# Fifteen checks with constants in place of a register loop, on four engines, for the spare expert blocks

## The reference, cut to what matters

```python
def grouped_expert_ffn(x2d, expert, gate, w_gate, w_up, w_down):
    # assignments sorted by expert, laid out in 128-row blocks that each belong to one expert
    ...
    def expert_block(args):
        xblk, e = args
        h = jax.nn.silu(xblk @ w_gate[e]) * (xblk @ w_up[e])
        return h @ w_down[e]
    yb = lax.map(expert_block, (xb, blk_expert)).reshape(cap, dm)
    y = yb[dest] * sgate[:, None]
    return jnp.zeros_like(x2d).at[stok].add(y)
```

## Time and profile before

| | before |
|---|---|
| median of 3 runs | 3962.31 us |
| span of the profiled execution, first to last instruction | 3962.9 us |
| instructions in it | 40374 |
| TensorE busy with matmuls | 3711.2 us, 94% of the span |
| VectorE, ScalarE, GpSimd busy | 42%, 19%, 4% |
| mean granted TensorE clock | 0.971 |

### The profile page before, as it was taken

One profiled execution on the slowest core, in us unless ns is written; L12 is line 12 of the kernel. 1 busy time (PEld: TensorE's weight loads), 2 busy tenths in 40 slices (PEclk: granted clock), 3 DMA queues, 4 the chain that ended last, 5 costly groups with the idle time before them and its releaser, 6 DMA issues. The chain is left out here.

```text
span 3962.9 us, 40374 instructions
## 1 busy us (share of the span) xinstructions
PE 3711.2 (94%) x15836; PEld 2158.0 (54%) x15836; DVE 1664.2 (42%) x2996; ACT 764.9 (19%) x1713; POOL 172.2 (4%) x393
## 2 busy tenths in 40 slices
PE   8988899989889999999789999999998999999999
PEld 4654787745344345555345454488444545448844
DVE  0118533555232011111445564554464655355435
ACT  1202211211132111000224352110002435110000
POOL 1001000000100000000202000000000200000000
PEclk9989999998999999999899999999999999999999
DMA  8542012223779887887441112222223110221221
GB/s 319 181 168 97 26 54 97 85 110 138 305 287 381 330 353 307 316 326 283 168 125 43 45 55 88 75 85 85 85 87 113 43 60 26 74 100 60 86 95 53
DMA packets 199024, 576.39 MB, mean 145 GB/s; under 512 B 24612, under 2 KB 34644, under 8 KB 185832
## 3 DMA queue, kind: packets, MB, share of 16 engines
q1 hardware_dynamic: 178064, 515.15, 34.8%
q10 hardware_dynamic: 12888, 32.14, 2.3%
q0 software_dynamic: 7888, 26.53, 1.9%
HBM read 541.80 MB, written 32.00 MB: 145 GB/s over the span
## 5 line engine op out<-in xcount | busy, mean ns | idle before, releaser
L346 PE MATMUL ps<-out_sums 128*128 128x256 f32 (+1 forms) x1152 | 333.6, 450 | 2.3 <-issue 2.3
L346 PEld LDWEIGHTS ps<-out_sums 128*128 128x128 f32 x1152 | 219.0, 190 | 113.9 <-issue 94.4
L346 PE MATMUL ps<-ring,mixers_xT 128*128 128x256 f32 (+2 forms) x1024 | 254.0, 403 | 14.1 <-DMA ring<-in_w_in 7.2
L346 PEld LDWEIGHTS ps<-ring,mixers_xT 128*128 128x128 f32 x1024 | 195.9, 201 | 61.3 <-issue 22.0
L346 PE MATMUL ps<-mixers_xT,ring 128*128 128x512 f32 (+1 forms) x480 | 209.2, 594 | 2.7 <-DMA ring<-in_w_in 1.7
L346 PE MATMUL ps<-ring,layers_hT 128*128 128x512 f32 x416 | 185.8, 604 | 17.2 <-PEq L276 16.2
L2307 PE MATMUL ps<-ring,mixers_xT 128*64 128x512 f32 x416 | 183.5, 598 | 2.1 <-issue 1.1
L346 PE MATMUL ps<-ring,ctx_hT 128*128 128x512 f32 (+2 forms) x448 | 168.9, 536 | 11.3 <-PEq L276 10.3
L2308 PE MATMUL ps<-ring,mixers_xT 128*64 128x512 f32 x400 | 176.5, 598 | 0.0
L346 PE MATMUL ps<-ring,out_hidden 128*128 128x512 f32 x384 | 167.4, 592 | 0.0
L346 PEld LDWEIGHTS ps<-mixers_xT,ring 128*128 128x128 f32 (+1 forms) x480 | 88.7, 187 | 117.5 <-issue 114.6
(11 more groups left out here) (857 smaller groups left out, 6042.7 us busy)
## 6 DMA issues: line engine op xcount, KB each, us to landing
ring<-in_w_ff SPq DMA_DIRECT2D x45, 2048.0 KB, 12.8
ring<-in_w_in SPq DMA_DIRECT2D x43, 2048.0 KB, 10.5
ring<-in_e_gate SPq DMA_DIRECT2D x28, 2048.0 KB, 15.7
ring<-in_e_down SPq DMA_DIRECT2D x27, 2048.0 KB, 9.2
ring<-in_e_up SPq DMA_DIRECT2D x25, 2048.0 KB, 11.7
ring<-in_w_ada SPq DMA_DIRECT2D x24, 2048.0 KB, 11.8
x_rows<-in_e_up SPq DMA_DIRECT2D x8, 2048.0 KB, 10.3
ring<-in_w_out SPq DMA_DIRECT2D x6, 2048.0 KB, 9.7
```

Of the source, the lines that this page charges most:

```text
L346: last = pe.matmul(out, lhsT, rhs, start=(j == 0), stop=(j == len(pairs) - 1))
```

## The change

In `blocks` the register loop becomes a loop of the program's author: fifteen branches and fifteen copies of the body for each of the four engines, with n a constant in each. GpSimd's part is as it was.

```diff
     def blocks(eng, body):
         used = eng.value_load(route.expert[0:1, SPARE:SPARE + 1], min_val=0, max_val=SPARE)
-        with eng.Fori(1, SPARE) as n:
-            with eng.If(n < used):
+        for n in range(1, SPARE):
+            with eng.If(used > n):
                 body(n)
```

## The result

The changed kernel takes 3981.5 us, the median of 5 runs (3975.92 to 3983.98); the kernel before, run beside it and counted with its earlier runs, 3965.75 us (3961.59 to 3967.95, 5 runs). The ratio is 1.0039, with a 95% interval of 1.0027 to 1.0051: slower by 0.39%, 15.8 us between the medians; the interval is 11 to 20 us. The forecast was 3976.7 us, +14.4.

The account below looks back on a forecast made before the run. TensorE's sequencer was taken to bound the stage between two barriers; its program fetches, 1914.5 + 6 x 3.5 = 1935.5 against 1921.1, add 14.4 us to the median 3962.3, giving 3976.7 us, range 3955 to 3983.

Parts of the forecast that it names:

- The bound: Stage between the barriers of L276 and L127: TensorE's sequencer arrives last at 1921.1 us, others 4 to 10 us early.
- The loop's own instructions: Spare-block checks: TensorE's turn of 0.78 us becomes a 0.29 us branch, 7.1 us earlier if nothing else happened.
- The allowance of up to two borders on queue 14: SyncE's and ScalarE's longer programs: at most two block borders, each 3 to 4.4 us, arriving at 1912 to 1920.
- Length: TensorE's fifteen skipped bodies: some 1875 instructions, 7.3 blocks of 256, eight borders, about seven more packets on queue 8.
- One block fetched ahead, each border a wait: TensorE's checks: first border free, next fetch there at 1914.5, six more one after another at 3.5 us each.
- The terms of the sum: TensorE's arrival at the stage's end: 1914.5 + 6 x 3.5 = 1935.5 us, 14.4 us later than 1921.1.
- What does not move: Next stage: TensorE's clock still starts at 0.50; loads in flight end by 1915.5 and are needed only behind the barrier.
- Fetches are waited for but short: Rival for TensorE's borders: 2.0 us a block gives +5.4 us, two fetched at once +3.9; chance 0.17.
- All there in time: Rival for TensorE's blocks: held or fetched many ahead, so -3 to -7.1 us; chance 0.28.
- Every skip a miss: Rival for TensorE's fifteen skips: each jump throws away what was fetched ahead, 66 us, 4028 us in all; chance 0.02.
- The change did what it says: Answers the rival that the loop was written out already; the prediction excluded it by 15 MOVEs, ALU_OPs and back branches.

Follow-up runs that it names:

- hollow: Changed kernel with TensorE's fifteen spare bodies cut to one wait and one semaphore instruction each, branches kept; one run, 3957.4 us.
- the half-length copies: Changed kernel with TensorE's spare bodies cut from 125 to 61 instructions, w_up and w_down products left out; one run, 3968.2 us.
- The two far jumps: Kernel before with TensorE's never-run body five times in its loop, 3973.6 us; changed kernel with its copies nested, one failing check leaving all, 3962.37 us.

## Why the prediction was right

*The bound.* TensorE's sequencer alone ends the stage: shown by keeping its loop, which restored 15.4 us, while three engines had the change.

*The loop's own instructions.* I gave the fifteen branches 0.29 us each; they take 0.28 in the changed kernel where no wait lies in them, 0.27 hollow. The other engines would arrive "at about 1911 to 1912": it was 1912.2 to 1913.3 in a stage that started 1.1 us later. The allowance of up to two borders on queue 14, 1912 to 1920, was too wide: three packets more moved and no branch of SyncE, ScalarE or VectorE took over 0.08 us.

*Length.* 125 instructions a body, 7.3 blocks, eight borders, the first free: 136 packets and seven waits came out as said. Eight packets lie in the stage, not 6 or 7, since the last block entered still sets off the next one.

*One block fetched ahead, each border a wait.* Shown by the packets, each of which starts only when the wait before it is over, by the half-length copies and by the hollow ones. The rule of the Trainium skill that the prediction quoted (Runtime: NRT & Kernel Launch, "Instruction fetch mechanics") lets a taken branch stall where its target's page is not among the two held. The two far jumps agree with it, 6.2 and 6.8 us. That every border is a stall does not follow from the rule alone, as I had it, for each jump over a border of the changed kernel lands in the very block that is being fetched ahead: it follows because a block is passed in 0.6 us and fetched in 3.3. The rule's window of two pages does not fit TensorE here: three blocks at least are held. The other figure quoted, 128 KB or eight blocks, is neither shown nor excluded as what is held; as what is fetched ahead it is excluded by the seven waits. Being held and being fetched ahead are two things, and only the second would have helped.

*The terms of the sum.* I had the first awaited block there 6.8 us after the stage's start, when its packet ends. The packet did end in time, at 1915.4, 6.6 us after the start, but the branch ended at 1916.8, 8.0 us after it: I had left out the 1.4 us between a block's landing and the next instruction. What they consist of stays open. Then six blocks at 3.5 us, 21 us; measured (1936.4 - 1916.8) / 6 = 3.3, 19.6 us. The first term was 1.2 us too small and the second 1.4 too large, so 27.6 us came out where I had 27.8. That the sum is so near is in part luck of two signs. A fetch over idle DMA engines has these parts in the trace's DMA records: 0.7 us, at times up to 1.4, from the jump into a block to the start of the next block's packet, 0.9 to 1.3 us of packet, and about 1.4 us more until the branch that waits for it goes on.

*The time.* The stage is 14.4 us longer, as forecast; the medians lie 15.8 us apart, and the 1.4 between is well inside the interval. The forecast of 3976.7 us is 4.8 us under the measured 3981.5. Of that 3.4 us come from the kernel before, whose median is 3965.75 us in 5 runs and was 3962.31 in the 3 that I added to. I had also taken the span of the profiled execution as its time; in the changed kernel's runs the time is 1.7 to 2.0 us above the span, so the profiled execution of before took some 3964.6 to 3964.9 us, 2.3 to 2.6 us above that median and not 0.6. The sum is a difference and doesn't change by it.

*What does not move.* The clock stood at 0.50 through the stage in both, and for 8.7 and 9.6 us behind it. TensorE's wait in front of L399, less the stage, is 6.6 us before and 6.7 after. Behind the barrier nothing but the clock's return was found to have moved, which is some 0.4 us of the 1.2 there.

*The rivals.* "Fetches are waited for but short", at 2.0 us a block or two fetched at once, fell: a block took 3.3 us, and no two packets overlap. "All there in time" fell, though its argument, the loop that crosses its border without a second fetch, was a true observation. "Every skip a miss" fell: every second one is, and with half the length one in four or five. The change did what it says: the changed kernel executes nothing on L2420.

## What to carry to other kernels

Writing a register loop out trades turns of 0.4 to 0.8 us for program that has to be fetched, and skipping code does not spare its fetch when the skips land in every block: count the instructions of all copies on TensorE, divide by 256, and put about 3.3 us on each block (more where loads fill the DMA engines) before counting the saved branches. Where the usual case skips everything, as with this data, one guard around the compact loop beats both forms. Data that uses the spare blocks, where the bodies are run, was not measured in any form. And ask first which engine arrives last: here three of four got faster for nothing.

## What the runs showed of the hardware that was not expected

A jump on TensorE is long in itself, 0.20 to 0.22 us when its target is there, against 0.05 us on SyncE and ScalarE, whatever its length: over the few instructions of a hollow body or over 630. The first jump into a block that is there already took 0.36 to 0.41 us. A jump to a block that is not there, one check behind the border before, waits 2.7 to 3.3 us over idle DMA engines (2.1 to 2.2 where three or four checks lay between) and 5.1 to 6.8 us while the 16 DMA engines are full with loads, although the packet itself takes 0.9 to 1.3 us in both. With full DMA engines the wait ended 8.1 to 8.5 us after the stage's start in all four traces that have one, wherever the jump stood.
